# Output stage of a hybrid layer: its seven products in another order

## The chip, the cores and the metric

One Trainium2 chip, one of its cores. The number reported is the device time of one launch in microseconds (us); for the kernel before it is the median of three runs. All rows below come from one profiled execution on that core; their times count from the start of its span.

## What is computed

`x` is 1024 frames of 2048 values. The layer normalises it, projects it, runs three groups of heads (16 units of 128 columns in all: a gated recurrence, band attention, retention), and then comes the part that this case is about:

```
y = jnp.concatenate([ya, yb, yc], axis=-1)          # (1, 1024, 2048)
return x + jnp.einsum('bse,ed->bsd', y, w_out)      # the output projection
...
return rmsnorm(x, final_gain)
```

## The kernel before

Everything is kept transposed: a row of `y_scratch` is one unit, 128 columns of y by 1024 frames. The output projection, y (2048) by w_out (2048 x 2048), is cut into 2 x 2 blocks and done by Strassen's seven products: weight blocks A11 to A22, y blocks B11 to B22, result blocks C11 to C22. In a y block (kb, sh), kb picks units 0 to 7 or 8 to 15 and sh the half of the frames. A product is a sum of one or two weight blocks times a sum of one or two y blocks, and is added to or taken from one or two blocks of the result.

A product has 8 steps, one for each pair of result rows (`PAIRS` = 8), so the stage has `STEPS` = 56. A step is 24 matmuls of 128x512 in two granules of 12 (four rows of weights, each times y in three products of high and low parts, since fp32 is split in an fp32r `w_hi`, `w_lo` and `mv_hi`, `mv_lo`). Granule n needs: its weights loaded by SyncE (SP), summed on GpSimd (POOL) if the product has two weight terms, the high part copied by ScalarE (`w_high`, L1595), the low part taken on VectorE (`weight_low`, L2220). There are four weight slots (`NG`), eight raw buffers of 256 KB (`RAWS`); SP reuses a raw buffer when the granule that used it is split. The y operands of a product ("combs", 8 of them) are loaded to `y_in`, summed on VectorE (`comb_add`, L2229), copied high by ScalarE (L1587), and taken low on VectorE (`comb_low`, L2238). One or two combs are made per step, always for the product after the present one; a product can't begin before its eighth comb is done. `accumulate(v)` (L2250) adds step v's PSUM bank to the result (in `arena`, which was loaded with x, the "residual"); there are four banks. `square` and `add_square` (L1602, L2263) build the sum for the last RMSNorm, `output_ss` (L1116) sums it over partitions, `scale_half` (L2275) writes the scaled half, from where SP stores it.

All queues are written out by hand, in the same loop on each engine: iteration v of VectorE is comb_add, add_square, comb_low, two weight_low (granules 2v+4 and 2v+5), accumulate(v).

The stage opens specially (`OPEN` = 4): steps 0 to 3 run first all with their first granule, then with their second. Before, their eight granules come through `w_sum` and both halves are split on POOL (L763, L765), and the operand of the first product (M3: B12 - B22) is made from 15 loaded half rows of y and the last unit by `first_sums`, `first_hi`, `first_los`. Row 7 of it needs the very last unit of y, so row 7 of steps 0 to 3 is done last.

## Time and profile before

| | |
|---|---|
| median of 3 runs | 1792.07 us (1791.39 to 1796.66) |
| profiled execution: its own time, its span | 1796.0 us, 1794.2 us |
| TensorE (PE) busy | 1744.9 us, 97% of the span |
| VectorE (DVE) busy | 1205.2 us, 67% |
| GpSimd (POOL) busy | 769.1 us, 43% |
| output stage, first matmul to last | 1458.2 to 1775.1 us |

How to read it: matmuls are pipelined, so a lone one is shown 0.39 us long while the next starts 0.23 us after it; idle time is counted from the shown end. Granted clock of TensorE is 1.00 throughout the stage.

### The profile page before, as it was taken

The numbers are of one execution on the slowest core, as the hardware profiler recorded it, in microseconds if no ns is written. First come the engines' busy times: TensorE is split into PE (matmuls) and PEld (weight loads), VectorE is DVE, ScalarE is ACT, GpSimd is POOL, SyncE is SP. The second block draws the span as 40 slices with busy tenths as digits, with TensorE's granted clock in tenths as the row PEclk, the third lists the DMA queues.
The fourth block names the chain that finished last, engine by engine and source line by source line (L and its number), as shares of the span: only waits on it lengthen the run. The fifth ranks groups of instructions, "written<-read, shape, count | busy, mean of one in ns | idle before, by whom it ended". The sixth has DMA issues, their size and how long they took to land.

```text
span 1794.2 us, 26920 instructions
## 1 busy us (share of the span) xinstructions
PE 1744.9 (97%) x10330; PEld 1441.6 (80%) x10330; DVE 1205.2 (67%) x1714; ACT 670.7 (37%) x972; POOL 769.1 (43%) x545
## 2 busy tenths in 40 slices
PE   7999999999999999999999999999999999999996
PEld 5888888888888788888888888888888877888874
DVE  6857665464678987887786355655654448777987
ACT  4423334333434344353343233333533223333442
POOL 4545444444454634444444433233433350355551
PEclk9999999999999999999999999999999999999998
DMA  7767778685987433233324333332433278678876
GB/s 248 234 225 256 242 231 263 214 273 186 297 270 244 148 106 96 89 96 112 89 83 136 90 108 107 97 95 86 150 109 109 86 249 307 236 235 261 286 238 223
DMA packets 160851, 323.29 MB, mean 180 GB/s; under 512 B 18378, under 2 KB 19151, under 8 KB 160724
## 3 DMA queue, kind: packets, MB, share of 16 engines
q1 hardware_dynamic: 146458, 276.52, 48.5%
q10 hardware_dynamic: 14266, 45.05, 7.3%
q8 instruction: 83, 1.36, 0.3%
q14 instruction: 44, 0.36, 0.1%
HBM read 275.35 MB, written 46.15 MB: 179 GB/s over the span
## 4 chain that ended last, share of the span: by engine, by line
PE 55%; DVE 6%; DMA 2%; issue 1%; ACT 1%; SPq 0%; POOL 0%; DVEq 0%; ACTq 0%
PE prj L811 33%; PE prj L1093 12%; PE mix L956 2%; PE mix L830 1%; PE mix L939 1%; DMA y_in<-y_scratch 1%; DVE arena L2275 1%; PE mix L949 1%; PE mix L882 1%; DVE w_lo L2220 1%; PE mix L909 1%; DVE arena L2250 1%; PE mix L912 1%; PE mix L898 1%; PE mix L987 0%
## 5 line engine op out<-in xcount | busy, mean ns | idle before, releaser
L763 POOL TENSOR_SCALAR w_hi<-w_sum 128x512 fp32r<-128x512 f32 x124 | 199.9, 1612 | 517.4 <-DMA w_sum<-in_w 498.1
L790 PE MATMUL prj<-in_hi,w_hi 128*128 128x512 f32 x840 | 329.2, 392 | 11.2 <-DVE w_lo L1685 9.5
L790 PE MATMUL prj<-in_lo,w_hi 128*128 128x512 f32 x840 | 327.5, 390 | 0.0
L790 PE MATMUL prj<-in_hi,w_lo 128*128 128x512 f32 x840 | 327.3, 390 | 0.0
L811 PE MATMUL prj<-mv_hi,w_hi 128*128 128x512 f32 x928 | 300.3, 405 | 0.0
L750 POOL TENSOR_TENSOR w_sum<-in_raw,in_raw 128x512 f32<-128x512 f32 x150 | 200.9, 1340 | 212.9 <-PE prj L790 200.8
L811 PE MATMUL prj<-mv_lo,w_hi 128*128 128x512 f32 x928 | 288.6, 392 | 0.0
L811 PE MATMUL prj<-mv_hi,w_lo 128*128 128x512 f32 x928 | 286.6, 390 | 0.0
L811 PEld LDWEIGHTS prj<-mv_hi,w_lo 128*128 128x128 f32 x928 | 174.5, 188 | 38.8
L811 PEld LDWEIGHTS prj<-mv_lo,w_hi 128*128 128x128 f32 x928 | 174.7, 188 | 38.4
L790 PEld LDWEIGHTS prj<-in_hi,w_hi 128*128 128x128 f32 x840 | 158.0, 188 | 46.8 <-issue 9.0
L1685 DVE TENSOR_TENSOR w_lo<-w_sum,w_hi 128x512 fp32r<-128x512 f32 x150 | 121.2, 810 | 108.3 <-ACT w_hi L1196 105.1
L811 PEld LDWEIGHTS prj<-mv_hi,w_hi 128*128 128x128 f32 x928 | 164.4, 189 | 29.0 <-issue 0.9
L790 PEld LDWEIGHTS prj<-in_lo,w_hi 128*128 128x128 f32 x840 | 158.1, 188 | 33.1 <-issue 0.5
L790 PEld LDWEIGHTS prj<-in_hi,w_lo 128*128 128x128 f32 x840 | 158.1, 188 | 33.1
L772 POOL TENSOR_TENSOR raws<-raws 128x512 f32<-128x512 f32 x80 | 112.3, 1406 | 166.8 <-DMA raws<-in_wo 166.8
L1093 PE MATMUL prj<-mv_hi,w_hi 128*128 128x512 f32 x448 | 175.6, 392 | 8.4 <-POOL w_lo L765 4.2
L1134 ACT ACTIVATE arena<-arena 128x1024 f32<-128x1024 f32 (+1 forms) x121 | 123.7, 1034 | 150.2 <-DVE arena L1791 126.0
L765 POOL TENSOR_TENSOR w_lo<-w_sum,w_hi 128x512 fp32r<-128x512 f32 x124 | 173.9, 1403 | 10.3
L1093 PE MATMUL prj<-mv_hi,w_lo 128*128 128x512 f32 x448 | 174.4, 389 | 0.0
L1093 PE MATMUL prj<-mv_lo,w_hi 128*128 128x512 f32 x448 | 174.4, 389 | 0.0
L1196 ACT ACTIVATE w_hi<-w_sum 128x512 fp32r<-128x512 f32 x150 | 94.2, 628 | 175.0 <-POOL w_sum L750 174.5
(177 smaller groups left out, 2463.2 us busy)
## 6 DMA issues: line engine op xcount, KB each, us to landing
in_raw<-in_wi SPq DMA_DIRECT2D x360, 256.0 KB, 3.3
raws<-in_wo SPq DMA_DIRECT2D x184, 256.0 KB, 3.6
w_sum<-in_w SPq DMA_DIRECT2D x116, 256.0 KB, 3.1
arena<-z_scratch ACTq DMA_DIRECT2D x56, 512.0 KB, 3.8
y_in<-y_scratch SPq DMA_DIRECT2D x80, 256.0 KB, 4.5
z_scratch<-acc_in SPq DMA_DIRECT2D x60, 256.0 KB, 3.9
z_scratch<-stage SPq DMA_DIRECT2D x26, 512.0 KB, 4.2
x_even<-in_xT SPq DMA_DIRECT2D x44, 256.0 KB, 4.0
```

What stands on the lines that cost most here:

```text
L750: nc.gpsimd.tensor_tensor(w_sum[wslot(n)][:], in_raw_buf(a), in_raw_buf(b), ALU.add if sign > 0 else ALU.subtract).then_inc(in_wsum, 1)
L763: nc.gpsimd.tensor_scalar(w_hi[q][:], w_sum[q][:], 1.0, None, ALU.mult).then_inc(w_hi_done, 1)
L765: nc.gpsimd.tensor_tensor(w_lo[q][:], w_sum[q][:], w_hi[q][:].bitcast(F32), ALU.subtract).then_inc(w_split, 1)
L772: nc.gpsimd.tensor_tensor(raw_buf(a), raw_buf(a), raw_buf(b), ALU.add if sign > 0 else ALU.subtract).then_inc(wsum_done, 1)
L790: last = nc.tensor.matmul(out, wt[wslot(n)][:, i % GRAN, :], mv[j % 2][:, i, :], start=(i == 0 and wt is w_hi and mv is in_hi), stop=(i == ...
L811: last = nc.tensor.matmul(prj[pair][:, half(side)], wt[wslot(q)][:, kk, :], mv[:, k, half(side)], start=(k == 0 and wt is w_hi and mv is m ...
L830: last = nc.tensor.transpose(mixb(n)[:, c, :], blocks(src)[:, c, :], ident[:])
L956: last = nc.tensor.matmul(mixb(1)[:, 5, :], blocks(V)[:, p + 1 - nk + j, :], blocks(BT[p % 2])[:, j, :], start=(j == 0), stop=(j == nk - 1))
L1093: last = nc.tensor.matmul(bank(s), wt[wslot(W0 + n)][:, i % GRAN, :], slot(mv, j, i), start=(i == 0 and wt is w_hi and mv is mv_hi), stop= ...
L1134: return nc.scalar.activation(out, src, ACT.Exp, **kw)
L1196: nc.scalar.activation(w_hi[wslot(n)][:], src, ACT.Copy).then_inc(in_w_hi, 1)
L1685: tt(w_lo[wslot(n)][:], src, w_hi[wslot(n)][:].bitcast(F32), ALU.subtract).then_inc(w_split, 1)
```

## The change

The products run in the order M2, M5, M1, M6, M7, M3, M4 instead of M3, M4, M1, M2, M5, M6, M7. With this:

- The first product (M2) takes eight single rows of y (units 0 to 7, first half of the frames), no sums and not the last unit. Its weights are A21 + A22, so the opening's eight granules each take two loads, a sum on POOL, a high copy on ScalarE and a low part on POOL.
- Steps 0 to 3 run their second granule whole.
- The weights of the last two products (M3, M4) are single; their low parts are taken on POOL (`out_low`), no longer on VectorE.
- The last two products each update two result blocks, so their squares come two per step, and the first half's scaling is spread over five steps.
- The residual is loaded a whole row at a time.

```diff
-PRODUCTS = [
-    ((A11,), 1, (B12, B22), -1, ((C12, 1), (C22, 1))),
-    ((A22,), 1, (B21, B11), -1, ((C11, 1), (C21, 1))),
...
-M3, M4, M1, M2, M5, M6, M7 = PRODUCTS
-IN_PRODUCTS = [M2, M5, M1, M6, M7, M3, M4]
+M1 = ((A11, A22), 1, (B11, B22), 1, ((C11, 1), (C22, 1)))
+M2 = ((A21, A22), 1, (B11,), 1, ((C21, 1), (C22, -1)))
+M3 = ((A11,), 1, (B12, B22), -1, ((C12, 1), (C22, 1)))
+M4 = ((A22,), 1, (B21, B11), -1, ((C11, 1), (C21, 1)))
+M5 = ((A11, A12), 1, (B22,), 1, ((C12, 1), (C11, -1)))
+M6 = ((A21, A11), -1, (B12, B11), 1, ((C22, 1),))
+M7 = ((A12, A22), -1, (B21, B22), 1, ((C11, 1),))
+PRODUCTS = [M2, M5, M1, M6, M7, M3, M4]
+TWO_TERM = 5 * 2 * PAIRS
...
+            sp.wait_ge(z_stored, 16 * (DIRECT - IN_TILES))
+            load_open_raw(0)
+            load_open_raw(1)
+            load_open_w(0)
+            load_open_w(1)
+            load_open_w(2)
+            sp.wait_ge(w_used, W0 - 1)
+            load_open_raw(2)
+            load_open_raw(3)
             sp.wait_ge(filled[1], M1_C + C_M1 * C_HEADS)
+            load_open_w(3)
             for p in range(2):
                 load_residual(p, 1, x2_in)
-            load_open_w(3)
+            load_open_raw(4)
+            load_open_w(4)
+            load_open_raw(5)
+            load_open_w(5)
+            for p in range(2, OPEN):
+                load_residual(p, 1, x2_in)
...
+            open_sum(0)
+            for n in range(1, 2 * OPEN):
+                open_sum(n)
+                out_low(n - 1)
+            out_low(2 * OPEN - 1)
+            for n in range(2 * OPEN, TWO_TERM):
...
+            pool.wait_ge(w_split, W0 + TWO_TERM)
+            for n in range(TWO_TERM, GRANULES):
+                out_low(n)
...
             for p in range(OPEN):
-                pe.wait_ge(w_split, W0 + OPEN + p + 1)
-                product(OPEN + p, p, range(GRAN, HK - 1))
-            for p in range(OPEN):
-                product(OPEN + p, p, [HK - 1]).then_inc(w_used, 1)
+                granule(OPEN + p, p, 1)
...
+            w_high(0)
             norm_first(1, M1_C + C_M1 * i + 3, m, A_HEADS + i)
+            w_high(1)
             norm_second(A_HEADS + i + 1)
+            w_high(2)
+            w_high(3)
             sigmoid(m, GATE)
...
-                if OPEN <= v + 2 < STEPS:
+                if v == OPEN - 2:
+                    dve.wait_ge(w_split, W0 + 2 * OPEN)
+                if 2 * OPEN <= 2 * v + 4 < TWO_TERM:
                     weight_low(2 * v + 4)
                     weight_low(2 * v + 5)
-                if v >= STEPS - 4:
-                    scale_half(1, 4 * (v - STEPS + 4), 4 * (v - STEPS + 4) + 4)
+                if v >= STEPS - 5:
+                    first = 3 * (v - STEPS + 5)
+                    scale_half(1, first + min(first, 1), first + 4)
                 accumulate(v)
```

Lines of VectorE (L2220 and on) and POOL have new numbers in the changed kernel: weight_low is L2246 there, accumulate L2276, comb_low L2264, add_square L2289, scale_half L2301.

VectorE from the last low part of the first operand (`mv_lo`, L2120) through iteration 4, before: four accumulations, then two weight low parts per iteration, then two combs.

```order
L2120 TENSOR_TENSOR mv_lo<-arena,mv_hi 128x512
L2250 TENSOR_TENSOR arena<-arena,prj 128x512 x4
L2220 TENSOR_TENSOR w_lo<-raws,w_hi 128x512 x2
L2250 TENSOR_TENSOR arena<-arena,prj 128x512 x2
L2220 TENSOR_TENSOR w_lo<-raws,w_hi 128x512 x2
L2250 TENSOR_TENSOR arena<-arena,prj 128x512 x2
L2229 TENSOR_TENSOR mix<-y_in 128x512 x2
L2238 TENSOR_TENSOR mv_lo<-mix,mv_hi 128x512 x2
L2220 TENSOR_TENSOR w_lo<-raws,w_hi 128x512 x2
L2250 TENSOR_TENSOR arena<-arena,prj 128x512 x2
```

The same place on VectorE in the changed kernel.

```order
L2276 TENSOR_TENSOR arena<-arena,prj 128x512 x4
L2246 TENSOR_TENSOR w_lo<-raws,w_hi 128x512 x2
L2276 TENSOR_TENSOR arena<-arena,prj 128x512 x2
L2246 TENSOR_TENSOR w_lo<-raws,w_hi 128x512 x2
L2276 TENSOR_TENSOR arena<-arena,prj 128x512 x2
L2258 MEMSET wait_pad 128x1 x2
L2264 TENSOR_TENSOR mv_lo<-y_in,mv_hi 128x512 x2
L2246 TENSOR_TENSOR w_lo<-raws,w_hi 128x512 x2
L2276 TENSOR_TENSOR arena<-arena,prj 128x512 x2
```

The order stays; the two sums into PSUM (`mix`) are gone, and the low part of a comb now reads both operands from SBUF (`y_in`).

POOL, which makes the opening's weights, before: high and low part of each granule, then 80 sums.

```order
L763 TENSOR_SCALAR w_hi<-w_sum_54 128x512
L765 TENSOR_TENSOR w_lo<-w_sum_54,w_hi 128x512
L763 TENSOR_SCALAR w_hi<-w_sum_55 128x512
L765 TENSOR_TENSOR w_lo<-w_sum_55,w_hi 128x512
L772 TENSOR_TENSOR raws<-raws 128x512 x80
```

POOL after: the sum of a granule (L793) stands ahead of the low part (L798) of the one before it.

```order
L793 TENSOR_TENSOR w_sum_57<-w_sum_57,raws 128x512
L798 TENSOR_TENSOR w_lo<-w_sum_56,w_hi 128x512
L793 TENSOR_TENSOR w_sum_54<-w_sum_54,raws 128x512
L798 TENSOR_TENSOR w_lo<-w_sum_57,w_hi 128x512
L793 TENSOR_TENSOR w_sum_55<-w_sum_55,raws 128x512
L798 TENSOR_TENSOR w_lo<-w_sum_54,w_hi 128x512
L798 TENSOR_TENSOR w_lo<-w_sum_55,w_hi 128x512
L811 TENSOR_TENSOR raws<-raws 128x512 x72
L798 TENSOR_TENSOR w_lo<-raws,w_hi 128x512 x32
```

Two POOL instructions per opening granule as before, but a low part now also waits for the next granule's loads, and 32 low parts of the last two products are new at the end of the queue.

VectorE at the very end, after (before, each L2250 stood alone, as did each L2263, and L2275 came in fours).

```order
L2301 SCALAR_TENSOR_TENSOR arena<-arena,fgain_sb,mix 128x512 x3
L2276 TENSOR_TENSOR arena<-arena,prj 128x512 x2
L2289 TENSOR_TENSOR mix<-mix,rstd 128x512 x3
L2289 TENSOR_TENSOR sum_sq_50<-mix,rstd 128x512
L2301 SCALAR_TENSOR_TENSOR arena<-arena,fgain_sb,mix 128x512 x16
```

Behind the last step there are now two accumulations and four additions of squares instead of one and two.

## Rows read from the trace of the kernel before

**Rows 1.** The page: busy time, share of the span and instructions of TensorE.

```profile
PE 1744.9 (97%) x10330; PEld 1441.6 (80%) x10330; DVE 1205.2 (67%) x1714; ACT 670.7 (37%) x972; POOL 769.1 (43%) x545
```

**Rows 2.** Waits of PE, 1458 us to the end: total, times, longest.

```profile
PE prj L1093 <- POOL w_lo L765: 4.2, 3, 2.3
PE prj L1093 <- DVE mv_lo L2238: 3.1, 3, 2.2
PE prj L1093 <- DVE arena L2250: 1.2, 1, 1.2
```

**Rows 3.** Timeline of PE: start, length, what, in brackets idle before and releaser.

```profile
1458.20 0.39 PE L1093 MATMUL prj<-mv_hi,w_hi 128*128 128x512 f32 x1
...
1471.35 0.39 PE L1093 MATMUL prj<-mv_hi,w_lo 128*128 128x512 f32 x1
1474.04 0.50 PE L1093 MATMUL prj<-mv_hi,w_hi 128*128 128x512 f32 x1 [2.30 <-POOL w_lo L765]
...
1486.87 0.47 PE L1093 MATMUL prj<-mv_hi,w_hi 128*128 128x512 f32 x1 [1.18 <-DVE arena L2250]
...
1640.25 0.47 PE L1093 MATMUL prj<-mv_hi,w_hi 128*128 128x512 f32 x1 [0.35 <-DVE mv_lo L2238]
...
1684.57 0.47 PE L1093 MATMUL prj<-mv_hi,w_hi 128*128 128x512 f32 x1 [0.51 <-DVE mv_lo L2238]
...
1730.59 0.47 PE L1093 MATMUL prj<-mv_hi,w_hi 128*128 128x512 f32 x1 [2.22 <-DVE mv_lo L2238]
...
1774.92 0.39 PE L1093 MATMUL prj<-mv_hi,w_lo 128*128 128x512 f32 x1
```

**Rows 4.** Chain that ended last: start, length, what.

```profile
1486.87 147.61 PE prj L1093 x648
```

**Rows 5.** Timeline of the opening: SP's issue, POOL, ScalarE.

```profile
1457.94 0.33 SPq L665 DMA_DIRECT2D w_sum<-in_wo  x1
1460.80 1.65 POOL L763 TENSOR_SCALAR w_hi<-w_sum 128x512 fp32r<-128x512 f32 x1 [1.61 <-DMA w_sum<-in_wo]
1452.52 1.03 ACT L1402 ACTIVATE arena<-mix 128x1024 f32<-128x1024 f32 x1 [5.29 <-PE mix L1012]
1458.40 0.63 ACT L1169 ACTIVATE part_hi<-arena 128x512 fp32r<-128x512 f32 x1 [4.20 <-PE mix L842]
```

**Rows 6.** Windows: busy PE, PEld, DVE, ACT, POOL, granted clock, DMA share, GB/s.

```profile
1500.00:1530.00 30.00, 30.00 (x133) 24.59 (x132) 23.48 (x39) 11.07 (x19) 0.00 (x0) 1.00 1.05 387
1685.00:1725.00 40.00, 40.00 (x178) 33.10 (x177) 36.08 (x49) 19.22 (x35) 19.89 (x16) 1.00 0.88 286
```

**Rows 7.** Groups, 1458 us to the end: busy us, mean ns, idle before.

```profile
L772 POOL TENSOR_TENSOR raws<-raws 128x512 f32<-128x512 f32 x80 | 112.3, 1406 | 166.8 <-DMA raws<-in_wo 166.8
L2220 DVE TENSOR_TENSOR w_lo<-raws,w_hi 128x512 fp32r<-128x512 f32 x104 | 93.7, 916 | 32.2 <-ACT w_hi L1595 32.1
L1595 ACT ACTIVATE w_hi<-raws 128x512 fp32r<-128x512 f32 x104 | 64.6, 627 | 72.6 <-PE prj L1093 72.4
L2229 DVE TENSOR_TENSOR mix<-y_in 128x512 f32<-128x512 f32 x32 | 23.0, 730 | 4.0 <-DMA y_in<-y_scratch 3.7
L2238 DVE TENSOR_TENSOR mv_lo<-y_in,mv_hi 128x512 fp32r<-128x512 f32 x16 | 18.5, 1158 | 11.4 <-ACT mv_hi L1587 11.4
```

**Rows 8.** Timeline of VectorE and POOL at 1611 us.

```profile
1611.31 1.63 DVE L2238 TENSOR_TENSOR mv_lo<-y_in,mv_hi 128x512 fp32r<-128x512 f32 x1 [0.71 <-ACT mv_hi L1587]
1614.08 1.28 DVE L2250 TENSOR_TENSOR arena<-arena,prj 128x512 f32<-128x512 f32 x2
1611.10 1.29 POOL L772 TENSOR_TENSOR raws<-raws 128x512 f32<-128x512 f32 x1 [2.25 <-DMA raws<-in_wo]
```

**Rows 9.** Timeline of the tail: VectorE, ScalarE.

```profile
1773.46 2.71 DVE L2275 SCALAR_TENSOR_TENSOR arena<-arena,fgain_sb,mix 128x512 f32<-128x512 f32 x4
1776.09 0.68 DVE L2250 TENSOR_TENSOR arena<-arena,prj 128x512 f32<-128x512 f32 x1
1776.80 0.63 ACT L1602 ACTIVATE rstd<-arena 128x512 f32<-128x512 f32 x1 [3.20 <-DVE arena L2250]
1777.48 0.69 DVE L2263 TENSOR_TENSOR sum_sq<-mix,rstd 128x512 f32<-128x512 f32 x1
```

More of the change, by code:

```diff
@@ L401, in build @@
         raw_of, raw_granule = {}, []
-        for n in range(2 * OPEN, GRANULES):
-            terms = PRODUCTS[n // 2 // PAIRS][0]
-            raw_of[n] = [len(raw_granule) + t for t in range(len(terms))]
-            raw_granule += [n] * len(terms)
+        for n in range(2, GRANULES):
+            loads = 1 if n < 2 * OPEN else len(PRODUCTS[n // 2 // PAIRS][0])
+            raw_of[n] = [len(raw_granule) + t for t in range(loads)]
+            raw_granule += [n] * loads
         in_raw_of, in_raw_granule = {}, []
@@ L682, in load_comb, with load_residual @@
                                  ).then_inc(ys_in[idx % YSLOTS], 16)
[L684 to L689 removed]
+            def load_residual(p, r, arrived):
+                sp.dma_start(acc_row(p, r), xT[2 * p + r]).then_inc(arrived[p // 2], 16)
+            sp.wait_ge(z_stored, 16 * (DIRECT - IN_TILES))
@@ L1617, in _ @@
                         square(q)
-                if v == STEPS - 5:
+                if v == STEPS - 6:
                     final_rms(1, 0)
-            square(len(squares) - 1)
+            for q, sq in enumerate(squares):
+                if sq[0] == STEPS:
+                    square(q)
             final_rms(0, 1)
@@ L2107, in _ @@
                 b_unit(i)
-            def first_sums(first, end):
-                for i in range(first, end):
-                    cur = arr(YS[i % 4])
-                    dve.wait_ge(yl_in[i % 4], 32 * (i // 4) + (32 if i < HK - 1 else 16))
-                    other = cur[:, half(1)] if i < HK - 1 else arr(Y)[:, half(1)]
-                    tt(cur[:, half(0)], cur[:, half(0)], other, ALU.subtract).then_inc(comb_sum, 1)
             def first_los(first, end):
```

150 lines of the change are left out of this document (71 added, 79 removed).

## Prediction, made before the changed kernel ran

> **What bounds the kernel now.** Start with the page: TensorE is busy for 97% of the span [rows 1], so only what it waits for, and what comes before its first or after its last matmul, can be won. The change touches the output stage alone, so read the waits of TensorE from 1458 us on [rows 2]. The reader is to see how little there is: seven waits, 4.2 + 3.1 + 1.2 = 8.5 us. The timeline says where they lie [rows 3]. Three are in the opening, for the weights' low parts from POOL, the first of 2.30 us. One of 1.18 stands ahead of step 4, for VectorE's accumulation: row 7 of steps 0 to 3 waits at the end of the opening, so all four steps end together. Three stand ahead of steps 32, 40 and 48, the first steps of M5, M6 and M7 (0.35, 0.51, 2.22), each for the low part of the last comb. Nothing else is lost: 648 matmuls take 147.61 us in one piece [rows 4], 0.2275 us each, so a step of 24 is 5.46 us. Each wait costs some 0.27 more than it shows. From 1471.35 to 1474.04 is 2.69; less the pitch 0.23 that is 2.46 against 2.30 shown, and the matmul behind it runs about 0.11 longer (0.50 against 0.39) [rows 3].
>
> So before, step 4 begins at 1486.87 and step 8 at 1486.87 + 4 x 5.46 = 1508.7. Without any wait, eight granules of 2.73 from 1458.20, and the two small matmuls between them (0.45), would bring step 4 to 1480.5. That is the most that the opening can give: 6.4 us, 0.36% of the time.
>
> **The opening's weights.** POOL still spends two instructions a granule, 1.4 us each [rows 7], so its work is not more. What is new is the second load, the ScalarE copies in a queue where other work waits, and that a low part stands behind the sum of the next granule. A load takes about 2.9 us: issued at 1457.94, used at 1460.80 [rows 5]. Slots still free one per finished granule. I follow them. Granule 3's weights are issued and land as before, its sum ends at 1462.2, and low part 2 at 1463.6, when TensorE wants it (1464.1). Weights 4 can be issued at 1461.1; ahead of them in the queue are six transfers of 256 KB (the residual of two pairs is four). At the best rate of the trace, 387 GB/s [rows 6], one takes 0.68 us, so they land at about 1464.7; sum 4 ends at 1466.1 and low part 3 at 1467.5, against 1466.8 wanted: 0.7 us of wait. In the same way low part 5 comes about 0.5 late, the other lows in time, and step 4 can begin at 1482.0, with 4.9 us won. The ScalarE copies 1 and 2 stand behind the copies that wait for TensorE (1452.52 and 1458.40 [rows 5]); they are ready before POOL asks. The last unit's y is stored some 3 us later, since the sigmoid stands behind copy 3, but the first comb that reads it is the eighth of M5, wanted at 1503, so I cost that at nothing. The y loads of ScalarE shrink from 15 to 8 and come earlier: no cost.
>
> **Where that gain goes.** Step 8 begins M5, and needs all eight combs of M5. VectorE makes two per iteration in 4 to 7. Follow VectorE. Weights 7 can be issued when granule 3 is done (1470.4), land at about 1473.6, and behind them on POOL stand sum 7, low part 6 and low part 7, which ends at 1477.8; then the sums of granules 8 to 11 follow. The raw loads of granule 11 reuse buffers that are free only after low part 7, and are the last of 15 transfers behind weights 7 (landed about 1473.6): 1473.6 + 15 x 0.68 = 1483.8. Sum 1.41, high copy 0.63 [rows 7], low 0.61, two accumulations 1.22 (two take 1.28 as shown, a pitch of 0.61 [rows 8]): VectorE begins iteration 4 at about 1487.5, that is 5.5 us after TensorE begins step 4. It is already late.
>
> An iteration then is: 0.12 for two markers, 0.71 of wait for ScalarE's first copy [rows 8], two comb lows from `y_in`, two weight lows, two accumulations (1.22). The lows take 0.61 each if POOL is silent. Before, it was: the products M3 and M4 have single weights, and POOL did nothing from 1500 to 1530 [rows 6]. Now it sums two granules a step there. What this does the trace shows later: the comb low at 1611.31 took 1.63 and ended when POOL's sum of 1611.10 to 1612.39 was over plus its own 0.6 [rows 8]. Mean is 1.158 for a comb low from `y_in`; for weight lows (93.7 - 24 x 0.68) / 80 = 0.97 once the first 24, made before POOL sums, are taken out [rows 7] at the 0.68 of a lone instruction [rows 9]. With 0.08 off for overlap: 0.12 + 0.71 + 2 x 1.08 + 2 x 0.89 + 1.22 = 6.0 us, against 5.46 for TensorE. Iteration 7 begins at 1487.5 + 18.0 = 1505.5 and its second comb low ends 3.0 later: step 8 at 1508.5, where it was 1508.7. The opening's 4.9 us are nearly all given back in one wait of some 4 to 5 us at step 8. With no contention at all the iteration is 4.5, VectorE catches up with TensorE, and step 8 begins at 1482.0 + 21.8 = 1503.8, for 4.9 us. If contention is half more, it is 1511. I take the row-mean: **-0.2**, bounds -4.9 and +3.
>
> The Trainium skill's GPSIMD Engine Reference (specifications) says the same of the cause: the SBUF interface is shared with VectorE, for instructions with two SBUF inputs. It gives no size; the rows do.
>
> **After step 8.** Gone are 0.35, 0.51 and 2.22 with 3 x 0.27: **-3.9**. The last of them came where VectorE had two lows, a comb and two squares per iteration. Now M6 and M7 have one accumulation and no squares, and M3 and M4 no weight lows, so step 48 should have no wait. New: M5, M1, M6 and M7 all run with weights of two terms and combs of two terms, as only M5 and M6 did before. M2 and M5, with two accumulations like M5 and M1 now, ended in waits of 0.35 and 0.51. I take 0.43 + 0.27 = 0.7 for steps 16 and 24 and 0.3 for 32 and 40: **+2.0** (0 to 6).
>
> Transfers: a step of M5 loads four raws, two y, two halves of x: 2.10 MB in 5.46 us, 384 GB/s. The trace held 387 for 30 us [rows 6]. So it just fits, at a VectorE pace that is no faster. The Trainium skill (DMA: Bandwidth & Descriptors, Specifications) puts the limit of a core at HBM near 358 GB/s; by that M5 would take 16.8 MB / 358 = 46.9 us instead of 43.7, 3.2 more. The trace disagrees, since 387 is above it.
>
> **The tail.** Before, the last matmul ends at about 1775.15; VectorE is then still scaling until 1776.09, accumulates once, and the last square's sum ends at 1778.17 [rows 9]: 3.0 us. Now the scalings are spread by threes and VectorE is free when the step ends: two accumulations (to +1.35), two waiting squares added (to +2.55), ScalarE's two squares between (each needs the addition two before it), the last two additions to +4.0: **+1.0**, bounds 0.5 and 2. The 16 scalings and stores behind are unchanged.
>
> **Sum.** -0.2 - 3.9 + 2.0 + 1.0 = -1.1 on the profiled execution's own 1796.0, so 1794.9. That execution lies 3.9 above the median of 1792.07, so the median should be **1791.0**. A change under 0.3%, 5.4 us, can't be told from none: faster is below 1786.7, slower above 1797.5.
>
> **Rivals.** *The opening's gain is kept.* VectorE and POOL fall into step, contention is small, step 8 at 1503.8: -4.9 - 3.9 + 1.5 + 1.0 = -6.3, **1785.8**. For it: a pair of VectorE's instructions that meets no POOL takes 1.28 [rows 8]. Against: VectorE starts iteration 4 late, and the mean is what it is. 0.2. *Loads come too late.* The place is the raw loads of granules 10 to 13 and then M5, whose buffers let SP run only four granules ahead. In 1685 to 1725 the trace had only 286 GB/s at a share of 0.88 [rows 6], which scales to 325 at full share. At 340 GB/s a step of M5 takes 6.2 us, 0.7 more, 5.7 in eight, less 2 of slack; and step 8 comes 3 later: -1.1 + 3.7 + 3 = +5.6, **1797.7**, slower. It decides from about 340 GB/s down. Against it: 387 with the same kinds of loads. 0.18. *The opening doesn't work as meant*: low parts 3 to 7 wait for ScalarE, whose queue holds four waits on TensorE and POOL, and TensorE stops as long as before (6 us). Since step 8 hangs on low part 7 and granule 11, each us there moves it: +2, **1793**, still no change. 0.12 of the forecast's side. The forecast itself, with step 8 where it was: 0.5.
>
> **Numbers.** Faster: the first rival's 0.2, of which 0.17 lies past the bound, and 0.03 of the forecast's spread. Slower: 0.17. The rest, 0.63, is within 0.3%. Range: from the first rival's value to just past the second's, taken a little wider on both sides for that, 1785 to 1799, leaves about 0.2 out.
>
> **What would show it.** Right: waits of TensorE in the opening sum to under 2.5 us and step 4 begins near 1482; one new wait of 3 to 6 us, for a comb's low part, at step 8; POOL's sums running in 1480 to 1510 and comb lows there over 1 us; no wait at step 48; four additions of squares between the last matmul and `output_ss`. Wrong: no wait at step 8; VectorE waiting for `y_in` or POOL for `raws` with TensorE behind them in M5; or a step 4 later than 1485.

## Result, and the profile after

The changed kernel takes **1803.92 us** (median of 10 runs, 1801.99 to 1806.23) against 1793.24 for the kernel before (10 runs beside it, 1790.93 to 1799.69). The ratio is **1.0056, 95% interval 1.0047 to 1.0064**: some 10 us slower. The forecast was 1791.0, its range 1785 to 1799.

The profiled execution took 1803.43, 0.5 below its median; that of before (1796.0) lies 2.8 above the 1793.24. So the two traces differ by only 7.4 us, and they can place no more than that. The page of the changed kernel, span and busy time (compare [rows 1]):

```profile
span 1801.6 us, 26906 instructions
PE 1747.7 (97%) x10330; PEld 1444.6 (80%) x10330; DVE 1191.4 (66%) x1674; ACT 673.4 (37%) x980; POOL 800.8 (44%) x569
```

Waits of TensorE from 1440 us to the end (total, times, longest; compare [rows 2]):

```profile
PE prj L1135 <- DVE mv_lo L2264: 7.9, 4, 4.9
PE mix L1155 <- DVE sum_sq L2289: 4.4, 1, 4.4
PE prj L1135 <- issue: 2.9, 3, 1.4
PE prj L1135 <- POOL w_lo L798: 1.9, 1, 1.9
```

Where they lie, from the timeline of TensorE (compare [rows 3]):

```profile
1466.43 0.47 PE L1135 MATMUL prj<-mv_hi,w_hi 128*128 128x512 f32 x1 [0.80 <-issue]
1474.01 0.50 PE L1135 MATMUL prj<-mv_hi,w_hi 128*128 128x512 f32 x1 [1.88 <-POOL w_lo L798]
1496.33 0.47 PE L1135 MATMUL prj<-mv_hi,w_hi 128*128 128x512 f32 x1 [1.38 <-issue]
1502.75 0.47 PE L1135 MATMUL prj<-mv_hi,w_hi 128*128 128x512 f32 x1 [0.72 <-issue]
...
1513.35 0.76 PE L1135 MATMUL prj<-mv_hi,w_hi 128*128 128x512 f32 x1 [4.88 <-DVE mv_lo L2264]
1513.91 0.63 PE L1135 MATMUL prj<-mv_lo,w_hi 128*128 128x512 f32 x1
1514.34 0.63 PE L1135 MATMUL prj<-mv_hi,w_lo 128*128 128x512 f32 x1
...
1559.61 0.47 PE L1135 MATMUL prj<-mv_hi,w_hi 128*128 128x512 f32 x1 [1.11 <-DVE mv_lo L2264]
1604.63 0.47 PE L1135 MATMUL prj<-mv_hi,w_hi 128*128 128x512 f32 x1 [1.23 <-DVE mv_lo L2264]
1649.15 0.47 PE L1135 MATMUL prj<-mv_hi,w_hi 128*128 128x512 f32 x1 [0.72 <-DVE mv_lo L2264]
```

They stand at granules 3 and 5 of the opening, at steps 6 and 7, and at steps 8 (4.88), 16, 24 and 32; at 40 and 48 there is none. The releaser "issue" means that the profile shows none; the waits at steps 6 and 7 end 0.1 behind the ends of VectorE's low parts of granules 12 and 14 (1496.23 and 1502.65), so VectorE is late there already. The matmuls behind the 4.88 run 0.43 apart instead of 0.23.

It is handier to count from the stage's first matmul (1458.20 before, 1456.86 after). In this table and the later one, a step's time is the start of its first matmul in the timeline, less that:

| us from the first matmul | before | after | difference added there |
|---|---|---|---|
| step 4 | 28.67 | 27.06 | -1.6 |
| step 8 | 50.62 | 56.49 | +7.5 |
| step 16 | 94.27 | 102.75 | +2.6 |
| step 48 | 272.39 | 279.44 | -1.4 |
| last matmul | 316.72 | 323.64 | -0.1 |
| end of the span | 336.0 | 344.8 | +1.8 |

That is 8.8, less 1.3 by which the stage began earlier: 7.4 (before rounding), the difference of the profiles. The loss lies between step 4 and step 16. VectorE there, iterations 4 to 7 (start, length, in brackets idle before and its releaser):

```profile
1490.48 0.07 DVE L2258 MEMSET wait_pad<- 128x1 f32 x2
1491.25 3.30 DVE L2264 TENSOR_TENSOR mv_lo<-y_in,mv_hi 128x512 fp32r<-128x512 f32 x2 [0.71 <-ACT mv_hi L1633]
1494.47 3.45 DVE L2246 TENSOR_TENSOR w_lo<-raws,w_hi 128x512 fp32r<-128x512 f32 x2
...
1499.07 0.07 DVE L2258 MEMSET wait_pad<- 128x1 f32 x2
...
1507.59 1.28 DVE L2276 TENSOR_TENSOR arena<-arena,prj 128x512 f32<-128x512 f32 x2
1510.86 0.06 DVE L2258 MEMSET wait_pad<- 128x1 f32 x1 [2.00 <-DMA y_in<-y_scratch]
...
1512.51 0.69 DVE L2264 TENSOR_TENSOR mv_lo<-y_in,mv_hi 128x512 fp32r<-128x512 f32 x1
```

Before, the same iterations began at these times (iteration 4, then 7):

```profile
1490.89 1.29 DVE L2229 TENSOR_TENSOR mix<-y_in 128x512 f32<-128x512 f32 x2
...
1506.03 1.30 DVE L2229 TENSOR_TENSOR mix<-y_in 128x512 f32<-128x512 f32 x2
1507.38 1.29 DVE L2238 TENSOR_TENSOR mv_lo<-mix,mv_hi 128x512 fp32r<-128x512 f32 x2
```

Counted from the first matmul, iteration 4 began at 32.69 before and 33.62 after, only 0.93 later. Iterations 4 to 6 took 15.14 before and 18.38 after, 3.24 more; from there to the end of the last comb's low part it was 2.64 and 4.34, 1.70 more. The three are the 5.9 by which step 8 came later than before, and the longer iterations, with the low parts under POOL's sums, are the largest of them.

POOL's sums that feed it:

```profile
1480.16 2.54 POOL L811 TENSOR_TENSOR raws<-raws 128x512 f32<-128x512 f32 x2 [2.49 <-DMA raws<-in_wo]
1484.12 1.29 POOL L811 TENSOR_TENSOR raws<-raws 128x512 f32<-128x512 f32 x1 [1.42 <-DMA raws<-in_wo]
1486.15 1.80 POOL L811 TENSOR_TENSOR raws<-raws 128x512 f32<-128x512 f32 x1 [0.74 <-DMA raws<-in_wo]
1491.01 6.37 POOL L811 TENSOR_TENSOR raws<-raws 128x512 f32<-128x512 f32 x4 [3.06 <-DMA raws<-in_wo]
```

And SyncE's issues there:

```profile
1483.27 15.48 SPq L680 DMA_DIRECT2D raws<-in_wo  x12
1498.80 0.90 SPq L688 DMA_DIRECT2D y_in<-y_scratch  x2
...
1504.48 0.91 SPq L688 DMA_DIRECT2D y_in<-y_scratch  x2
```

POOL waits for the raws of granules 8, 10, 11 and 12. Twelve raw loads take SyncE 15.48 us, since those of granule n may go only when low part n-4 is taken; the y rows of combs 4 to 7 stand behind them. Each of these needs a free slot of `y_in` too, for combs 6 and 7 those of 2 and 3, whose low parts ended at 1501.44 and 1502.05. The last pair is issued at 1504.48 and has VectorE wait until 1510.86. VectorE's waits for `y_in` from 1486 to 1560:

```profile
DVE wait_pad L2258 <- DMA y_in<-y_scratch: 2.0, 1, 2.0
DVE mix L2255 <- DMA y_in<-y_scratch: 1.9, 2, 1.5
```

Windows (columns as in [rows 6]):

```profile
1475.00:1480.00 5.00, 5.00 (x16) 3.96 (x15) 1.29 (x2) 0.63 (x1) 2.67 (x3) 0.66 0.99 363
1480.00:1485.00 5.00, 5.00 (x23) 4.14 (x23) 2.63 (x4) 1.26 (x2) 3.42 (x3) 1.00 1.06 402
1485.00:1490.00 5.00, 5.00 (x23) 4.14 (x23) 2.33 (x5) 1.26 (x2) 2.20 (x2) 1.00 1.03 394
...
1495.00:1500.00 5.00, 3.67 (x16) 3.10 (x17) 4.29 (x7) 0.82 (x2) 2.78 (x3) 1.00 0.48 137
1510.00:1515.00 5.00, 1.65 (x4) 1.39 (x5) 3.24 (x8) 2.30 (x4) 1.15 (x2) 0.78 1.04 400
```

The DMA engines are full to 1490 and half idle behind it (137 GB/s), when SyncE has work but may not issue it. And TensorE's granted clock falls twice, behind the waits of 1474.01 and 1513.35. The 0.66 and 0.78 are means of 5 us; from 1476 to 1478 and from 1513 to 1516 it is 0.50, the lower of its two levels. Before, it was 1.00 throughout.

The tail (compare [rows 9]; the last matmul starts at 1780.50):

```profile
1780.92 1.28 DVE L2276 TENSOR_TENSOR arena<-arena,prj 128x512 f32<-128x512 f32 x2 [0.78 <-PE prj L1135]
1782.12 2.30 DVE L2289 TENSOR_TENSOR mix<-mix,rstd 128x512 f32<-128x512 f32 x3
...
1784.53 0.69 DVE L2289 TENSOR_TENSOR sum_sq<-mix,rstd 128x512 f32<-128x512 f32 x1
1785.28 1.52 PE L1155 MATMUL mix<-sum_sq,ones 128*128 128x512 f32 x2 [4.39 <-DVE sum_sq L2289]
```

### The profile page after: what moved, and what is told of

The parts are those of the page before. It is cut to its first block, busy times and chain, and to the rows that moved or that the text cites. A ratio compares the mean times of both kernels' runs of the same rounds, so it can differ in the third digit from the quotient of the medians.

```text
span 1801.6 us, 26906 instructions
## 1 busy us (share of the span) xinstructions
PE 1747.7 (97%) x10330; PEld 1444.6 (80%) x10330; DVE 1191.4 (66%) x1674; ACT 673.4 (37%) x980; POOL 800.8 (44%) x569
## 4 chain that ended last, share of the span: by engine, by line
PE 53%; DVE 7%; DMA 3%; issue 2%; ACT 1%; SPq 1%; POOL 0%; DVEq 0%; ACTq 0%; POOLq 0%
PE prj L853 33%; PE prj L1135 9%; DMA y_in<-y_scratch 2%; PE mix L998 2%; DVE w_lo L2246 1%; PE mix L872 1%; PE mix L981 1%; PE mix L991 1%; DVE mv_lo L2264 1%; PE mix L924 1%; DVE arena L2276 1%; PE mix L951 1%; ACT mv_hi L1633 1%; DVE arena L2301 1%; PE mix L954 1%
## 5 line engine op out<-in xcount | busy, mean ns | idle before, releaser
L781 POOL TENSOR_SCALAR w_hi<-w_sum 128x512 fp32r<-128x512 f32 x116 | 186.9, 1611 | 491.9 <-DMA w_sum<-in_w 491.9
L783 POOL TENSOR_TENSOR w_lo<-w_sum,w_hi 128x512 fp32r<-128x512 f32 x116 | 165.1, 1423 | 9.7
L1235 ACT ACTIVATE w_hi<-w_sum 128x512 fp32r<-128x512 f32 x150 | 94.3, 629 | 181.7 <-POOL w_sum L768 181.5
L811 POOL TENSOR_TENSOR raws<-raws 128x512 f32<-128x512 f32 x72 | 101.6, 1415 | 101.3 <-DMA raws<-in_wo 100.8
```

Source lines behind the costliest of these rows:

```text
L781: nc.gpsimd.tensor_scalar(w_hi[q][:], w_sum[q][:], 1.0, None, ALU.mult).then_inc(w_hi_done, 1)
L783: nc.gpsimd.tensor_tensor(w_lo[q][:], w_sum[q][:], w_hi[q][:].bitcast(F32), ALU.subtract).then_inc(w_split, 1)
L811: nc.gpsimd.tensor_tensor(raw_buf(a), raw_buf(a), raw_buf(b), ALU.add if sign > 0 else ALU.subtract).then_inc(wsum_done, 1)
L1235: nc.scalar.activation(w_hi[wslot(n)][:], src, ACT.Copy).then_inc(in_w_hi, 1)
```

## Experiments

The theory at the start: VectorE makes M5's eight combs too late, by three things that add up: raws that land late, y rows that stand behind gated raws in SyncE's queue, and low parts under POOL's sums. All kernels in one table; "step 8" and "step 16" are of the one profiled execution, the ratio is to the kernel before, run beside it on the same chip. Medians of different rows are of different chips, so the ratios are to be compared.

How far a single profile can be trusted: e7 and e12 have the same program as the changed kernel up to the end of step 7. Their iteration 4 began at 32.4 and 33.7 (33.6), and step 8 at 53.8 and 55.3 (56.5). So step 8 moves by 2.7 from one execution to another, and what the table shows of it below that is not told from chance. Of e1 to e8, only e6 has a ratio whose interval lies clear of the changed kernel's. e2, e5, e11, e12 and e14 leave out sums, loads or a square, as said with each, so that they compute something else; they serve for the times alone.

| | median, runs | ratio, 95% interval | step 8 | step 16 |
|---|---|---|---|---|
| before | | 1 | 50.6 | 94.3 |
| after | 1803.92, 10 | 1.0056 [1.0047, 1.0064] | 56.5 | 102.8 |
| e1 early combs | 1804.47, 4 | 1.0075 [1.0047, 1.0104] | 57.0 | 102.3 |
| e2 no sums in M2 | 1801.18, 6 | 1.0045 [1.0032, 1.0058] | 52.5 | 100.7 |
| e3 raws first | 1801.49, 8 | 1.0046 [1.0032, 1.0060] | 53.0 | 99.9 |
| e4 PSUM copy | 1805.61, 4 | 1.0065 [1.0046, 1.0085] | 56.3 | 102.7 |
| e5 small residual | 1801.47, 6 | 1.0040 [1.0026, 1.0054] | 53.3 | 100.7 |
| e6 deadline order | 1800.00, 6 | 1.0034 [1.0022, 1.0046] | 53.2 | 100.2 |
| e7 kept busy | 1802.80, 4 | 1.0050 [1.0035, 1.0065] | 53.8 | 101.0 |
| e8 e6 + early combs | 1801.09, 5 | 1.0041 [1.0028, 1.0054] | 57.2 | 103.3 |
| e9 combs a step sooner | 1803.38, 6 | 1.0052 [1.0039, 1.0066] | 48.0 | 98.2 |
| e10 e9 kept busy | 1800.86, 5 | 1.0041 [1.0028, 1.0054] | 51.4 | 99.5 |
| e11 e9, small residual | 1801.29, 4 | 1.0051 [1.0031, 1.0071] | 48.8 | 98.0 |
| e12 three squares | 1805.69, 4 | 1.0066 [1.0046, 1.0087] | 55.3 | 103.7 |
| e13 e9, y rows first | 1795.67, 12 | 1.0005 [0.9995, 1.0015] | 49.2 | 95.5 |
| e14 e13, no sums in M5 | 1793.22, 10 | 0.9993 [0.9983, 1.0004] | 49.1 | 94.3 |
| e15 e13, a step of room | 1790.92, 9 | 0.9979 [0.9969, 0.9989] | 49.3 | 93.4 |
| e16 before, a step of room | 1791.01, 11 | 0.9979 [0.9970, 0.9987] | 50.6 | 94.2 |

**e1: y rows of combs 4 to 7 ahead of the raws.** They go to halves of `y_in` that M5 leaves free.

```diff
             sp.wait_ge(y_stored, 16 * (UNITS + 1))
+            for idx in range(YSLOTS, HK):
+                load_comb(idx)
             for p in range(OPEN + 2, PAIRS):
...
-            more_combs = {8: (4, 5), 9: (6, 7)}
+            more_combs = {}
```

> The changed kernel with one move in SyncE's queue: the y rows of M5's combs 4 to 7 are issued right after the last unit is stored, ahead of the raw loads that wait for weight low parts, into the second halves of y_in. In the changed kernel step 8 began 56.5 us after the stage's first matmul (50.6 before). Theory (queue): combs 4 to 7 stand behind gated raw loads and land some 2 us too late, so VectorE's wait of 2.00 for y_in at 1510.86 goes and step 8 begins about 54.5; time 2 to 3 us below the changed kernel, about 1801. Rival (contention: POOL's sums stretch VectorE's low parts): VectorE's iterations stay 6 us or more, step 8 stays between 56 and 57, time the same within 0.5 us. Rival (saturated DMA): six more transfers ahead of the raws make POOL wait longer and step 8 comes later than 56.5.

VectorE's wait for `y_in` went, but POOL now waited 6.41 for the raws of granule 12, and step 8 came at 57.0. The 6.41 is what the third outcome named, four transfers more ahead of those raws. They gave nothing at step 8; that 57.0 is later than 56.5 one profile can't tell. At step 6 TensorE waited 3.81, and the matmuls behind it ran 0.43 apart for 4.8 us.

**e2: no sums on POOL for granules 8 to 15.**

```diff
+                if n < 2 * PAIRS:
+                    nc.gpsimd.memset(sum_pad[...], 0.0).then_inc(wsum_done, 1)
+                    continue
```

> The changed kernel, but POOL leaves out its sums for granules 8 to 15 (steps 4 to 7 of M2 then multiply by A21 alone); the loads and every wait stay, and a tiny memset stands for each sum. Theory (contention and POOL's own time): without POOL's eight sums of 1.4 us VectorE's low parts take 0.6 each there, an iteration 4.5 instead of 5.3 to 8.6, and step 8 begins 3 to 5 us earlier, 51.5 to 53.5 after the first matmul; time 1799 to 1801. Rival (late loads): the raws land when they land, VectorE's long iteration from 1490.48 to 1499.07 stays, step 8 gains under 1.5 us. If both are at work the gain is 1.5 to 3.

Step 8 came 4.0 earlier than in the changed kernel and 1.3 earlier than in e7. Iteration 4 took 6.8 us instead of 8.6 (7.7 in e7 and e12). So the sums cost something, as the prediction had it, though the two ratios' intervals overlap; and TensorE still waited 4.60 at step 8, so they are not all.

**e3: raws 8, 9, 10 ahead of the residual,** and raws 11 ahead of the y rows, whose lines stand behind those shown.

```diff
-            for p in range(OPEN, OPEN + 2):
-                load_residual(p, 1, x2_in)
             load_raw(2 * OPEN)
             load_raw(2 * OPEN + 1)
+            load_raw(2 * OPEN + 2)
+            for p in range(OPEN, OPEN + 2):
+                load_residual(p, 1, x2_in)
+            load_raw(2 * OPEN + 3)
```

> The changed kernel with another order of transfers on SyncE: the raws of granules 8 to 10 go first, then the residual of pairs 4 and 5, raws 11, then combs 0 to 3. Theory (the raws of granules 10 and 11 are late, POOL waited 0.74 and 3.06 for them): the sums of granules 10 and 11 come 1 to 3 us earlier, VectorE's iteration 4 begins by 1489 instead of 1490.5 and step 8 at 54.5 to 55.5 (56.5 in the changed kernel); time 1 to 2 us lower. Rival (buffers free only after low part 7, so the order does nothing for granule 11, and combs 0 and 1 come later): step 8 stays within 0.5 of 56.5, or comes later.

VectorE's iteration 4 began at 1486.02, 30.5 after the first matmul (33.6 in the changed kernel, 32.4 in e7), and step 8 came 3.5 earlier (0.8 earlier than in e7). Behind that, POOL waited 5.64 for the raws of granule 12. The order of equal bytes moves the start of iteration 4 by some 2 to 3 us; a gain in time the ratio does not show.

**e4: the comb lows read PSUM.** ScalarE writes a second copy of each of M5's y rows to `mix`.

```diff
+                if idx < HK:
+                    nc.scalar.activation(slot(mv_hi, 1, idx), src, ACT.Copy).then_inc(comb_hi, 1)
+                    nc.scalar.activation(mix[0][:, half(idx % 2)], src, ACT.Copy).then_inc(comb_copy, 1)
+                    return
...
-                src = mix[0][:, half(idx % 2)] if len(y_terms(idx)) == 2 else y_buf(idx, 0)
+                src = mix[0][:, half(idx % 2)]
```

> The changed kernel, but for M5's eight combs ScalarE writes a second copy of the y row to PSUM and VectorE's comb low part reads this and the high part, so only one of its inputs is in SBUF, as before. POOL, the loads and the weights' low parts are as in the changed kernel. Theory (contention on SBUF for instructions with two SBUF inputs): the eight comb lows of M5 fall from 1.1 to 1.9 us to about 0.7, each iteration loses 1 us less, less 0.6 for ScalarE's extra copy; step 8 begins 1 to 3 us earlier (54 to 55.5), time 1801 to 1803. Rival (loads or queue): comb lows shrink but VectorE then waits longer for y_in or ScalarE, step 8 within 0.5 of 56.5, the time unchanged.

The comb lows took 0.69 each, even under POOL's sums (in the changed kernel two took 3.30 and 2.21), so an input in PSUM does take them out of the contention. But VectorE then waited 1.26 and 0.35 for the copies, and step 8 stayed at 56.3. The rival came true: it is no cure.

**e5: only an eighth of the residual of pairs 4 to 7.**

```diff
+                if r == 1 and p >= OPEN:
+                    sp.dma_start(acc_row(p, r)[:, 0:P], xT[2 * p + r][:, 0:P]).then_inc(arrived[p // 2], 16)
+                    return
```

> The changed kernel, but of the residual rows of pairs 4 to 7 only 128 of 1024 columns are loaded (64 KB for 512 KB; the other columns of those rows of the output lack x). All sums, waits and the order stay: only 1.8 MB fewer pass the DMA engines between 1475 and 1495. Theory (backlog: with 16 raw loads, 8 y rows and 4 MB of residual the engines are full from 1475 to 1490, 402 and 394 GB/s, so the raws of granule 12, issued near 1483, land 7 to 8 us later): they land up to 1.8 MB / 395 GB/s = 4.6 us earlier, POOL's wait of 3.06 at 1491.01 goes, VectorE's iteration 4 takes 6 instead of 8.6, and step 8 begins 52.5 to 54 us after the first matmul (56.5 in the changed kernel); time 2 to 4 below it, about 1801. Rival (VectorE's low parts under POOL's sums): the data come early, the iterations stay at 6 us or more, step 8 at 55.5 to 56.5.

The sum of granule 12 began 31.1 after the first matmul (34.2 in the changed kernel), and step 8 came at 53.3, both as the backlog's theory says. But iteration 4 took 7.7 where 6 was expected, VectorE waited 1.52 for `y_in`, and 53.3 is only 0.5 from e7's place.

**e6: loads in the order of need.**

```diff
+            load_raw(8); load_raw(9); load_raw(10)
+            load_comb(0); load_comb(1)
+            load_residual(4, 1, x2_in); load_residual(5, 1, x2_in)
+            load_raw(11); load_raw(12); load_raw(13)
+            load_comb(2); load_comb(3)
+            load_raw(14)
+            load_residual(6, 1, x2_in); load_residual(7, 1, x2_in)
+            load_raw(15)
```

> The changed kernel with SyncE's loads for steps 4 to 7 in the order in which they are wanted: raws 8, 9, 10, combs 0 and 1, residual 4 and 5, raws 11, 12, 13, combs 2 and 3, raws 14, residual 6 and 7, raws 15. The bytes are the same. In the changed kernel, and in the version with raws first, 4 to 6 transfers of 256 KB that are wanted only later stand ahead of raws 12. Theory (backlog): raws 12 land 2 to 3.5 us earlier than the 1490 of the changed kernel, VectorE's iteration 4 is near 6 us, step 8 begins at 51.5 to 53; time 1799 to 1801. Rival (full engines as such, whatever the order): something else is late by as much, step 8 stays near the 53.0 that raws first gave or behind it.

The ratio is 0.22% below the changed kernel's. Iteration 4 took 5.5 us, as the theory has it, though it began at 33.2, no earlier than in the changed kernel. But step 8 is at 53.2, where e3 was, outside the forecast 51.5 to 53: now POOL waited 3.37 for raws 11, and VectorE waited 1.84 and 0.64 for the y rows of combs 6 and 7.

**e7: TensorE kept busy in the wait at step 8.**

```diff
+                if s == PAIRS:
+                    for k in range(16):
+                        last = nc.tensor.matmul(mix[0][:, half(0)], ones[:], slot(mv_hi, 0, 0),
+                                                start=(k == 0), stop=(k == 15))
+                    last.then_inc(kept_busy, 1)
```

> The changed kernel with 16 matmuls of 128x512 more (all-ones weights times an old high part, into PSUM that nobody reads) between steps 7 and 8, in the place of the wait for M5's last comb: 16 x 0.23 = 3.7 us inside a wait of 4.9. In the changed kernel the first matmuls of step 8 ran 0.43 apart for 2.1 us (granted clock 0.78), which costs about 1.3 us. Theory (the clock falls because TensorE stood still): the clock stays 1.00 there, step 8 to 9 takes 5.5 instead of 6.9, time 1 to 2 us below the changed kernel, about 1802.5. Rival (the low clock has nothing to do with that wait): step 8 to 9 stays at 6.5 to 7 and the time is that of the changed kernel.

The timeline of e7, and a window of it:

```profile
1507.35 3.79 PE L1162 MATMUL mix<-mv_hi,ones 128*128 128x512 f32 x16
1511.64 0.47 PE L1136 MATMUL prj<-mv_hi,w_hi 128*128 128x512 f32 x1 [0.50 <-DVE mv_lo L2272]
```

```profile
1510.00:1515.00 5.00, 4.50 (x21) 3.40 (x20) 3.84 (x7) 1.75 (x4) 2.19 (x2) 1.00 1.05 405
```

The clock stayed at 1.00, and step 8 took 5.56 instead of 6.90. So in this execution busy matmuls in place of the wait kept the clock. That supports the theory that the wait brings it down: all twelve traces with a wait of 3.81 to 6.89 in the stage have 0.43 between matmuls behind it. The time is 1.1 lower, within what these intervals can't tell.

**e8: e6 and e1 together.**

```diff
             load_comb(2); load_comb(3)
+            load_comb(4); load_comb(5)
             load_raw(14)
             load_residual(6, 1, x2_in); load_residual(7, 1, x2_in)
             load_raw(15)
+            load_comb(6); load_comb(7)
```

> The deadline order together with M5's combs 4 to 7 in the second halves of y_in, issued behind combs 2 and 3 and behind raws 15, ahead of the raws that wait for weight low parts. Theory (backlog first, then the queue): the deadline order makes iteration 4 short, and then VectorE's waits for y_in in iterations 6 and 7 (0.3 and 1.0 in the version with raws first) are what is left; without them step 8 begins at 50.5 to 52 and the time is 1798 to 1800. Rival (early combs only add to the backlog, as when they were moved alone: step 8 at 57.0): step 8 no earlier than in the deadline order alone.

Step 8 came at 57.2, and the sum of granule 11 began at 30.5 (28.3 in e6): the rival. Early y rows gave nothing, as long as VectorE makes the combs no sooner; the ratio is that of e6 within the intervals.

**e9: M5's combs in iterations 3 to 6,** with e1's slots and an order like e6's.

```diff
-            if OPEN <= v < PAIRS:
-                return [2 * (v - OPEN), 2 * (v - OPEN) + 1]
+            if OPEN - 1 <= v < PAIRS - 1:
+                return [2 * (v - OPEN) + 2, 2 * (v - OPEN) + 3]
```

> The deadline order, M5's combs 4 to 7 in the second halves of y_in, and M5's eight combs made in iterations 3 to 6 of VectorE instead of 4 to 7, so that a late iteration has one step (5.5 us) of room before step 8. Theory (what is lost is the lateness of VectorE's comb iterations against TensorE, made of late raws, of y rows behind gated raws and of iterations that cannot be shorter than a step): the wait at step 8 goes or falls under 1 us, step 8 begins 47.5 to 49.5 us after the stage's first matmul (53.0 to 53.3 in the three best versions so far, 56.5 in the changed kernel, 50.6 before), no half clock there, and the time is 1793 to 1796. Rival (full DMA engines: the stage cannot run ahead of its transfers): step 8 comes near 48 but TensorE then waits as long at steps 5 to 7 or 9 to 16, step 16 stays at 99 or later (100 before this), the time at 1799 or above.

Step 8 came at 48.0, with 0.95 of wait where 4.88 had been, and it made the time no better: TensorE now waits 5.6 at step 16. Its waits, and VectorE's from 1486 to 1560:

```profile
PE prj L1146 <- DVE mv_lo L2275: 6.5, 3, 5.6
...
DVE mix L2266 <- DMA y_in<-y_scratch: 7.6, 7, 2.6
```

The theory was right for step 8 and wrong for the time, the rival's waiting at step 16 came true. (This profile is of the fastest of the six runs, 4.2 below their median.)

**e10: e9 with 12 extra matmuls ahead of step 8,** e7's edit.

> The same with 12 matmuls more (2.7 us) ahead of step 8, as in the kept-busy run. Theory: if no wait is left at step 8, these matmuls are simply 2.7 us of work in the way and the time is 2 to 3 us longer than without them. Rival: if a wait of 3 us or more is left there (the transfers' rival), they cost nothing and save the half clock, so the time is 1 us shorter or the same.

Step 8 moved by 3.4, step 16 by 1.3 only; the time did not grow. What is ahead of step 16 was waiting anyhow.

**e11: e9 with 3.7 MB less to load in M5,** e5's edit under `if r == 0`.

> The version with combs made one step sooner, but of the residual rows that M5 needs (the other half of the rows) only 128 of 1024 columns are loaded, 64 KB for 512 KB (those rows of the output lack x in the other columns): 3.7 MB fewer in M5's eight steps, everything else as it is. In that version step 8 came at 48.0 us after the first matmul and a wait of 5.6 stood at step 16, which came at 98.2; steps 8 to 16 asked for 16.8 MB. Theory (the first sixteen steps of the new order are bound by their transfers: some 32 MB at 392 GB/s): 3.7 MB are 9.4 us, so the wait at step 16 falls from 5.6 to under 2 and step 16 comes at 93 to 95; time 3 to 4 below that version, 1799 to 1800 against 1803. Rival (VectorE and POOL set the pace of M1's combs): step 16 stays at 97 to 98.5.

The DMA engines moved 287 GB/s in the 45 us from 1508 (351 in e9), and step 16 did not move: 98.0. So full engines are not what binds M5. That theory fell.

**e12: one square less in the tail.**

```diff
+            if v == STEPS:
+                return [(p, C11)]
             return [(p, C21), (p, C11)] if j == 6 else []
```

> The changed kernel, but the square of the last row of C21 is left out of the last sum of squares (the first half's scale is off by that row): three additions instead of four behind the last matmul. In the changed kernel the sum over partitions starts 4.78 us after the start of the last matmul and takes 1.52 for its two matmuls; before it was 3.31 and 1.13. Theory (the tail is the chain of additions, and TensorE's clock falls when it stands still a little longer): start at 4.0 to 4.2, and with the shorter wait 1.13 again; tail from last matmul to the end 20.0 to 20.4 instead of 21.1. Rival (ScalarE's squares set the pace): start under 0.3 earlier. The time itself changes by under 1 us, which no run here can tell.

The sum over partitions started 3.97 after the last matmul (4.78), so the chain of additions sets it. But its two matmuls took 2.06, behind a shorter wait; the clock is not as simple as that wait.

```profile
1788.88 2.06 PE L1157 MATMUL mix<-sum_sq,ones 128*128 128x512 f32 x2 [3.59 <-DVE sum_sq L2291]
```

**e13: in M5 and later, the y row ahead of the raws, and a step sooner.**

```diff
             for s in range(PAIRS, STEPS):
+                if HK <= s - 1 < Y_COMBS:
+                    load_comb(s - 1)
                 load_raw(2 * s)
                 load_raw(2 * s + 1)
-                for idx in more_combs.get(s, ()):
-                    load_comb(idx)
```

> The version with combs made one step sooner, and from step 9 on each y row of a later comb is issued on SyncE ahead of the two raw pairs of its step and one step sooner, so it no longer stands behind raw loads that wait for a weight low part. There and in its small-residual variant VectorE waited 0.6 to 2.6 us for y_in in most of iterations 8 to 15, and the wait at step 16 was 5.6 and 4.0. Theory (SyncE's queue: y rows behind gated raws make VectorE late, in M5 as in M2): these waits for y_in go, step 16 comes at 93 to 95 us after the first matmul (98.2 and 98.0), the time is 1796 to 1799. Rival (VectorE's lows under POOL's sums and the ring of eight raw buffers set a pace of 5.7 a step): the waits for y_in turn into waits for raws, step 16 stays at 97 or later.

**1.0005 against 1.0052 for e9: the loss is gone.** Step 16 came at 95.5, not quite the 93 to 95 of the theory, with a wait of 2.6 left there. All of VectorE's waits from 1486 to 1560 in e13, with none for `y_in` left:

```profile
DVE mv_lo L2273 <- ACT mv_hi L1642: 8.1, 12, 0.7
DVE w_lo L2255 <- ACT w_hi L1597: 4.6, 5, 1.8
```

The waits did not turn into waits for raws (POOL waited 35.7 us for these in that stretch, and 36.2 in e9), although the same bytes now pass at a higher rate, 380 GB/s at a share of 1.03 from 1505 to 1550. The Trainium skill (DMA: Bandwidth & Descriptors, Specifications) has about 358 GB/s as HBM's limit for a core; by it, as an estimate, these 45 us could carry 1 MB less. The measurement decides.

The traces of e9 and e13 differ by only 3.2 us at the last matmul, e9's being of its fastest run; the rest of the 0.47% stands in the ratios alone.

**e14: e13 without POOL's sums in M5,** e2's edit under `if 16 <= n < 32`.

> The same kernel, but POOL leaves out its sums for granules 16 to 31 (M5 then multiplies by A11 alone); loads and waits stay, a tiny memset stands for each sum. Theory (y rows behind gated raws are what made M5 late): with that gone, the sums matter little, step 16 within 1 us of the version with sums. Rival (contention and the ring): without the sums VectorE's two lows take 1.28 each time instead of 2.4 or more, and raw buffers turn round 1.4 sooner, so step 16 comes 2 to 4 us earlier than with them.

Step 16 came 1.2 earlier, and the wait of 0.84 at step 24 went too. The ratio is 0.12% lower with intervals that overlap, against 0.47% for the queue: in M5 the sums are the smaller cause of the two.

**e15: one step of room for every product's combs.**

```diff
-            return [v] if PAIRS <= v < Y_COMBS else []
+            if v < PAIRS or v >= Y_COMBS or v % PAIRS == PAIRS - 1:
+                return []
+            return [v, v + 1] if v % PAIRS == 0 else [v + 1]
```

> The version with y rows first in SyncE's queue, and now every later product's combs are made one step sooner too: two in the first step of the product before, none in its last. Theory (a comb made in the very step before it is wanted leaves no room; a late VectorE becomes a wait at the product's first step): the waits at step 16 (2.6) and 24 (0.8) go, step 16 comes at 93 us after the first matmul (95.5), step 48 at 268 to 270 (272.4; 272.4 before the change), the time is 1791 to 1793.5, and the ratio to the kernel before is 0.998 to 1.0005. Rival (VectorE's average pace under POOL's sums is the bound, not its room): the waits only move to other steps, the time stays at 1795 to 1796.

**e16: the kernel before, with the same room.** The same edit of `combs_at`, and y rows loaded a step sooner, from step 16 on ahead of the raws.

> The kernel before (the old order of products) with that same step of room for the combs of its third to last products, and y rows ahead of the raws from step 16 on. It had waits of 0.35, 0.51 and 2.22 at steps 32, 40 and 48. Theory: they go, 3.9 us, and the time is 1789 to 1791, ratio 0.997 to 0.999; the room is then worth the same in either order, and the new order with room is not faster than the old one with it. Rival (the new order is the better one once its loads are in order): this one gains less than 1 us, the new order with room ends below it.

In e15 step 16 came at 93.4 and step 48 at 267.5, in e16 step 48 at 268.3: both theories came true, e15 slightly below its forecast places. Waits of TensorE from 1452 on, first e15, then e16:

```profile
PE mix L1168 <- DVE sum_sq L2302: 4.4, 1, 4.4
PE prj L1148 <- issue: 2.5, 2, 1.6
PE prj L1148 <- POOL w_lo L811: 1.8, 1, 1.8
```

```profile
PE prj L1101 <- POOL w_lo L773: 3.4, 3, 2.0
PE mix L1124 <- DVE sum_sq L2271: 2.9, 1, 2.9
PE prj L1101 <- DVE arena L2258: 1.2, 1, 1.2
...
```

No wait for a comb's low part is left in either. Both kernels beat both of this case, by 0.21% of before, and neither order of products is ahead of the other: the new one begins step 16 0.8 earlier and takes 1.15 more from the start of its last matmul on (21.39 to 20.24). Both edits give room and issue y rows a step sooner; which of the two does it was not tested.

## Why the prediction was wrong

**The step that failed** is the term for step 8, **-0.2 with bounds of -4.9 and +3; it measured +5.9** (+3.2 and +4.7 in e7 and e12, still outside). Counted from the first matmul, VectorE's iteration 4 was to begin at 29.3 and began at 33.6 (1490.48). The three iterations 4 to 6 were to take 18.0 and took 18.4: the contention with POOL was sized well in sum, though it came as 8.6, 5.3 and 4.5 and not as three times 6.0. Then iteration 7 was to reach its second comb low's end in 3.0 and took 4.3, with 2.00 of wait for `y_in`. So 4.3 + 0.4 + 1.3 = 6.0 of the 6.2 by which step 8 missed its forecast place are placed.

- *The 4.3: raws.* "1473.6 + 15 x 0.68" counted transfers, but had all of them issued by then. SyncE issued raws 11 only from 1476.56 to 1478.03, and POOL could begin their sum at 29.3 where 25.6 was forecast. Two rows of residual and three y rows stood ahead of them. With raws 11 ahead of the y rows (e3) their sum began at 26.6 and iteration 4 at 30.5, with an eighth of the residual (e5) at 27.2 and 31.5. In the three traces with the changed kernel's queue it began at 32.4 to 33.7, so some 1 to 3 us of the 4.3 hang on it. e6 left the start where it was and shortened the iteration instead.
- *The 1.3: SyncE's queue.* The prediction named a wait for `y_in` only as something that would show it wrong, and never followed where combs 4 to 7 stand in that queue: behind twelve raws, each gated by a low part. With combs and y rows sooner in M2 alone the loss moved on to step 16, with 7.6 us of waits for `y_in` (e9); e13 differs from e9 in nothing but the y rows' place from step 9 on, and is 0.47% lower. So the two together remove the loss. How much of the changed kernel's own 10 us the queue is, they don't show: there VectorE waited 3.9 for `y_in` up to 1560, and y rows first without the earlier combs was not tried.
- *The clock,* in no term of the sum: 1.6 behind the wait that ends at 1474.01, and 1.3 in step 8.

**The second rival, loads that come too late,** had the right side and much of the place (late raws, then M5) and the wrong mechanism: it wanted a transfer rate of 340 GB/s or less. The rate was 402 and 394 GB/s up to 1490 and 360 from 1505 to 1550, and 3.7 MB less changed nothing in M5 (e11). Its price of 1797.7 was too low.

**The opening** was to bring step 4 to 23.8 after the first matmul (1482.0); it came at 27.1. Waits of 2.7 instead of 1.2, and the clock. Against before it gained 1.6, not 4.9.

**After step 8.** The waits at 40 and 48 went as predicted. The new ones were 1.11, 1.23 and 0.72 and none, 3.1 with 3 x 0.27 = 3.9 where 2.0 stood; still within 0 to 6. So this term was near in number, and the credit of -3.9 in it was not owed to the order of products: e16, the old order with room, loses the same waits.

**The tail:** +1.0 forecast, +1.8 measured. The additions ended at 1784.53 + 0.69 = 1785.22, 4.5 after the last step's end (1780.50 + 0.23) where 4.0 was told, and 0.4 is the slower pair of matmuls (1.52 for 1.13).

**Left open.** The traces differ by 7.4 us, the medians by 10.7. What the other 3 are was not found; that the profile of before is one of its slower executions accounts for it in number, not in place. How the loss divides among late raws, low parts under POOL's sums, y rows in the queue and the clock is not shown beyond the bounds above, since single profiles of the same code differ by 2.7 at step 8. Why the granted clock falls behind 1.88 us of wait in the changed kernel, and did not behind 2.30 before or 3.32 at e1's step 8, stays open.
